# Scale and shift of a norm folded into the modulation behind it, and two moved steps in the MLP, in a two-layer transformer block kernel

## The reference

```python
y = concat(mixer) @ w_out
x = layer_norm(DEEPNORM_ALPHA * x + g_a * y, ln1_g, ln1_b)
h = x * (1 + sc_m) + sh_m
m = square(relu(h @ mlp_w1)) @ mlp_w2            # 1024 -> 4096 -> 1024
x = layer_norm(DEEPNORM_ALPHA * x + g_m * m, ln2_g, ln2_b)
```

## Time and profile before

| | us |
|---|---|
| runs, median (lowest to highest) | 3045.91 (3042.36 to 3052.49) |
| the profiled execution | 3046.93 |
| its span, first to last instruction | 3045.1 |
| PE busy | 2802.1 (92%) |
| DVE busy | 1397.4 (46%) |
| ACT busy | 878.6 (29%) |
| POOL busy | 559.6 (18%) |
| mean granted TensorE clock | 0.959 |

### The profile page before, as it was taken

The page is one execution under the profiler, slowest core; times in us unless marked ns, Lnnn a source line. Parts: engine busy times, 40 slices in busy tenths (PEclk is TensorE's granted clock), DMA queues, the critical chain, the costliest instruction groups (busy, mean ns, idle before and its releaser), DMA issues. The chain is left out here.

```text
span 3045.1 us, 40518 instructions
## 1 busy us (share of the span) xinstructions
PE 2802.1 (92%) x15572; PEld 2288.9 (75%) x15572; DVE 1397.4 (46%) x2153; ACT 878.6 (29%) x1684; POOL 559.6 (18%) x375
## 2 busy tenths in 40 slices
PE   5999993999999999999957999999698999999997
PEld 2666783778888888888845888888576888888886
DVE  3575435563333333333383555555555433333345
ACT  4243323342111121121224344343433211121222
POOL 0000002232112121121140000000033323233231
PEclk6999996999999999999977999999999999999999
DMA  6575214541101011010033111110356111111112
GB/s 219 195 301 166 73 52 158 165 132 49 35 28 55 28 41 41 28 55 28 30 122 96 42 36 49 36 36 8 105 131 173 48 46 44 55 41 41 55 41 56
DMA packets 192607, 238.90 MB, mean 78 GB/s; under 512 B 15960, under 2 KB 153776, under 8 KB 186352
## 3 DMA queue, kind: packets, MB, share of 16 engines
q1 hardware_dynamic: 192208, 237.29, 24.4%
q10 hardware_dynamic: 288, 0.10, 0.0%
HBM read 203.70 MB, written 37.88 MB: 79 GB/s over the span
## 5 line engine op out<-in xcount | busy, mean ns | idle before, releaser
L2054 DVE TENSOR_TENSOR y<-y,pair 128x1024 f32<-128x1024 f32 x280 | 340.1, 1219 | 314.1 <-PE pair L2161 314.1
L2159 PE MATMUL pair<-m_wbh,m_ath 128*128 128x512 f32 x1152 | 452.6, 393 | 15.0 <-DVE y L2054 8.4
L2161 PE MATMUL pair<-m_wbh,m_atl 128*128 128x512 f32 x1152 | 451.2, 392 | 0.0
L2160 PE MATMUL pair<-m_wbl,m_ath 128*128 128x512 f32 x1152 | 450.0, 391 | 0.0
L2103 DVE TENSOR_TENSOR m_atl<-m_sq,m_ath 128x512 fp32r<-128x512 f32 x160 | 138.4, 866 | 664.9 <-POOL m_sq L1972 664.0
L1932 ACT ACTIVATE m_rel<-pair 128x512 f32<-128x512 f32 x160 | 88.9, 556 | 996.7 <-PE pair L2183 986.3
L1972 POOL TENSOR_TENSOR m_sq<-m_rel 128x512 f32<-128x512 f32 x160 | 155.7, 973 | 1138.1 <-ACT m_rel L1932 1137.9
L2181 PE MATMUL pair<-hth,m0n_wah 128*128 128x512 f32 (+1 forms) x768 | 273.0, 355 | 2.8 <-ACT m_rel L1932 2.8
L2182 PE MATMUL pair<-htl,m0n_wah 128*128 128x512 f32 (+1 forms) x768 | 273.3, 356 | 0.0
L2183 PE MATMUL pair<-hth,m0n_wal 128*128 128x512 f32 (+1 forms) x768 | 273.2, 356 | 0.0
L2159 PEld LDWEIGHTS pair<-m_wbh,m_ath 128*128 128x128 f32 x1152 | 216.7, 188 | 70.1 <-DVE y L2054 16.8
(11 more groups left out here) (256 smaller groups left out, 5158.5 us busy)
## 6 DMA issues: line engine op xcount, KB each, us to landing
a_ring<-in_w_mod SPq DMA_DIRECT2D x40, 1024.0 KB, 9.1
m_rawb<-in_mlp_w SPq DMA_DIRECT2D x64, 512.0 KB, 4.2
m_rawa<-in_mlp_w SPq DMA_DIRECT2D x60, 512.0 KB, 4.2
x_rows<-r_res SPq DMA_DIRECT2D x28, 512.0 KB, 3.1
r_raw<-cat_cols SPq DMA_DIRECT2D x18, 512.0 KB, 6.0
mod_w<-in_w_mod SPq DMA_DIRECT2D x8, 1024.0 KB, 12.2
r_xin<-in_x SPq DMA_DIRECT2D x16, 512.0 KB, 3.6
gate_pre<-a0g_gout SPq DMA_DIRECT2D x20, 256.0 KB, 2.0
```

What stands on the lines that cost most here:

```text
L2054: dve.tensor_tensor(k.y[:, t, :], k.y[:, t, :], k.pair[t % 2][:, :], ALU.add).then_inc(s_y, 1)
L2159: pe.matmul(o, ath[:, m, ts], wbh[:, m, cols], start=m == 0, stop=False)
L2160: pe.matmul(o, ath[:, m, ts], wbl[:, m, cols], start=False, stop=False)
L2161: i = pe.matmul(o, atl[:, m, ts], wbh[:, m, cols], start=False, stop=m == M - 1)
```

## The change

The transposes no longer wait for POOL's two operations, but for the normed row alone, and the scale and shift of the norm are folded once per layer into the modulation's columns: scale' = (1 + sc) g, shift' = sh + (1 + sc) b. The two vectors are loaded as 16 rows, transposed by PE and applied by four small DVE operations. POOL still makes the row that is stored, but now in place only once the transposes have read it (a wait for `s_tr`). The last tile's transposes stand behind the first half of group 0 in `step(0)`. In layer 1 the first two `w2` pieces are loaded ahead of the rows of `y`, `begin_y` does two tiles ahead of the last `split_ht` instead of six, and POOL's gating stands ahead of all groups of a chunk. The last chunk of layer 1 leaves the loop: each group's `second(15, g)` follows its first product, with its `w2` parts in other buffers (`endh`, `endl`), and sums, squares and finishes are spread over both groups (four slots of `fmv` and `fstd` instead of two).

```diff
-        with eng.Fori(1, NCH) as c:
+        with eng.Fori(1, NCH - 1 if final else NCH) as c:
             body(c)
+        if final:
+            body(NCH - 1)
+
+    ends = lambda c: final and isinstance(c, int) and c == NCH - 1
+
+    def nth(c, t):
+
+        if not (final and isinstance(c, int) and c >= NCH - 2):
+            return tiles * c + t
+        g = [g for g in range(NG) if t in tiles_of(g)][0]
+        first, count = tiles_of(g)[0], len(tiles_of(g))
+        return tiles * (NCH - 2) + 2 * first + (c - (NCH - 2)) * count + t - first
...
+            for i, name in enumerate(("ln1_g", "ln1_b")):
+                sp.dma_start(lnr[i * KT:(i + 1) * KT, :], io[name][layer].rearrange("(k p) -> k p", p=P)).then_inc(s_lnr, 16)
...
+                    sp.wait_ge(s_dve, C * t + 2)
+                    for m in range(M):
+                        sp.dma_start(rawb[:, m, :], w2[m * P:(m + 1) * P, :]).then_inc(s_rawb[m], 16)
...
+                    if final and starts(c):
+                        continue
...
+                act.wait_ge(s_fold, 4)
...
+                if ends(c):
+                    act.wait_ge(s_alow, M * NCH)
+                    for m in range(M):
+                        act.wait_ge(s_bg, M * c + m + 1)
+                        act.activation(endh[:, m, :], rawb[:, m, :], ACT.Copy).then_inc(s_bhigh, 1)
...
-                    if g == NG - 1:
+                    if g == NG - 1 and not ends(c):
...
+                    if ends(c):
+                        act.wait_ge(s_sq, J * c + M * (g + 1))
+                        act.wait_ge(s_ath, J * c + M * (g + 1))
+                        for t in tiles_of(g):
+                            spread(t)
...
                 pool.wait_ge(s_dve, C * t + 6)
+                pool.wait_ge(s_tr, t + 1)
...
+                if final:
+                    for m in range(M):
+                        if starts(c):
+                            pool.wait_ge(s_grow, 16)
+                        wait(pool, s_rawb[m], 16 * (c + 1))
+                        pool.tensor_tensor(rawb[:, m, :], rawb[:, m, :], growt, ALU.mult).then_inc(s_bg, 1)
                 for g, (a, n) in enumerate(groups):
-                    if final and g == NG - 1:
-                        for m in range(M):
-                            if starts(c):
-                                pool.wait_ge(s_grow, 16)
-                            wait(pool, s_rawb[m], 16 * (c + 1))
-                            pool.tensor_tensor(rawb[:, m, :], rawb[:, m, :], growt, ALU.mult).then_inc(s_bg, 1)
...
+            scale, shift = [k.mod[:, layer, part * KT:(part + 1) * KT, :] for part in (SC_M, SH_M)]
+            column = lambda i: lnc[:, i, :].unsqueeze(2).broadcast_to([P, KT, 2])
+            dve.wait_ge(s_lnt, 1)
+            dve.tensor_copy(lnc[:, :, :].rearrange("p i j -> p (i j)"), k.bank[7][:, 0:2 * KT]).then_inc(s_fold, 1)
+            dve.wait_ge(s_fold, 1)
+            dve.tensor_tensor(lnt[:, :, :], scale, column(1), ALU.mult).then_inc(s_fold, 1)
+            dve.wait_ge(s_fold, 2)
+            dve.tensor_tensor(shift, shift, lnt[:, :, :], ALU.add).then_inc(s_fold, 1)
+            dve.tensor_tensor(scale, scale, column(0), ALU.mult).then_inc(s_fold, 1)
...
-            begin_y(0 if final else 2, XT - 2 if final else XT)
+            begin_y(0 if final else 2, 2 if final else XT)
             split_ht(tiles - 1)
-            begin_y(XT - 2 if final else XT, tiles)
+            begin_y(2 if final else XT, tiles)
...
+            def ending(c):
+                dve.wait_ge(s_lnrow, 32)
+                late = []
+                for g, (a, n) in enumerate(groups):
+                    for t in tiles_of(g):
+                        sum_tile(c - 1, t)
+                        if late and t > tiles_of(g)[0]:
+                            finish(late.pop(0))
+                    if g == 0:
+                        for m in range(M):
+                            dve.wait_ge(s_bhigh, M * c + m + 1)
+                            dve.tensor_tensor(endl[:, m, :], rawb[:, m, :], f32(endh[:, m, :]), ALU.subtract).then_inc(s_blow, 1)
+                    for m in range(M):
+                        j = J * c + g * M + m
+                        dve.wait_ge(s_sq, j + 1)
+                        dve.wait_ge(s_ath, j + 1)
+                        dve.tensor_tensor(atl[:, m, a:a + n], sq[:, m % 2, 0:n], f32(ath[:, m, a:a + n]), ALU.subtract).then_inc(s_atl, 1)
+                    for t in tiles_of(g):
+                        moments_sum(t)
+                        late.append(t)
+                        if len(late) > (2 if g < NG - 1 else 1):
+                            finish(late.pop(0))
+                for t in late:
+                    finish(t)
...
-                pe.wait_ge(s_b, t + 1)
+                pe.wait_ge(s_dve, C * t + 6)
...
+            pe.wait_ge(s_lnr, 32)
+            pe.transpose(k.bank[7][:, 0:2 * KT], lnr[:, :], k.ident[0:2 * KT, 0:2 * KT]).then_inc(s_lnt, 1)
...
-                        if g == 1:
-                            transposes(tiles - 1)
...
+                        if starts(c) and jj == 1:
+                            transposes(tiles - 1)
...
+                    if ends(c):
+                        second(c, g)
```

More of the change, by code:

```diff
@@ L1728, in stage_block @@
     s_dve, s_std, s_g, s_b, s_tr, s_mod, s_hh, s_hl, s_half = [rsem(x) for x in ("dve", "std", "g", "b", "tr", "mod", "hh", "hl", "half")]
+    s_lnr, s_lnt, s_fold = rsem("lnr"), rsem("lnt"), rsem("fold")
     s_store = [rsem(f"store{i}") for i in range(2)]
@@ L1934, in step, with spread @@
                         act.activation(ath[:, m, a:a + n], rel[:, m % 2, 0:n], ACT.Square).then_inc(s_ath, 1)
-            over_steps(act, step)
[L1936 to L1943, removed]
+                    if ends(c):
[3 more added lines that the diff above has]
+                            spread(t)
+            def spread(t):
+                act.wait_ge(s_mom, t + 1)
+                act.activation(rel[:, :, :].rearrange("p a b -> p (a b)"), k.y[:, t, :], ACT.Square, bias=fmv[:, t % 4, 0:1],
+                               accum_out=fmv[:, t % 4, 1:2]).then_inc(s_centre, 1)
+                act.wait_ge(s_centre, t + 1)
+                act.activation(fstd[:, t % 4, 0:1], fmv[:, t % 4, 1:2], ACT.Sqrt, bias=k.eps[:, 0:1], scale=1.0 / D).then_inc(s_fstd, 1)
+            over_steps(act, step)
         @block.gpsimd
@@ L2044, in _ @@
             split_ht(tiles - 2)
-            begin_y(0 if final else 2, XT - 2 if final else XT)
+            begin_y(0 if final else 2, 2 if final else XT)
             split_ht(tiles - 1)
-            begin_y(XT - 2 if final else XT, tiles)
+            begin_y(2 if final else XT, tiles)
             def sum_tile(c, t):
-                n = tiles * c + t
-                wait(dve, s_w2, n + 1)
-                wait(dve, s_y, n + 1)
+                wait(dve, s_w2, nth(c, t) + 1)
+                wait(dve, s_y, tiles * c + t + 1)
                 dve.tensor_tensor(k.y[:, t, :], k.y[:, t, :], k.pair[t % 2][:, :], ALU.add).then_inc(s_y, 1)
@@ L2069, in moments_sum @@
             def moments_sum(t):
-                n = tiles * (NCH - 1) + t
+                n = nth(NCH - 1, t)
                 dve.wait_ge(s_w2, n + 1)
-                dve.wait_ge(s_y, n + 1)
-                if t >= 2:
-                    dve.wait_ge(s_fstd, t - 1)
+                dve.wait_ge(s_y, tiles + nth(NCH - 2, t) + 1)
+                if t >= 4:
+                    dve.wait_ge(s_fstd, t - 3)
                 dve.tensor_tensor_reduce(k.y[:, t, :], k.y[:, t, :], k.pair[t % 2][:, :], 1.0, 0.0,
@@ L2077, in moments_sum @@
                 dve.wait_ge(s_y, tiles + n + 1)
[L2078 removed]
+                dve.tensor_scalar(fmv[:, t % 4, 0:1], stats[:, t % 2, 0, 0:1], -1.0 / D, None, ALU.mult).then_inc(s_mom, 1)
             def finish(t):
@@ L2082, in finish @@
                 dve.wait_ge(s_centre, t + 1)
-                dve.scalar_tensor_tensor(out=y, in0=y, scalar=fmv[:, t % 2, 0:1], in1=lng2, op0=ALU.add, op1=ALU.mult).then_inc(s_res, 1)
+                dve.scalar_tensor_tensor(out=y, in0=y, scalar=fmv[:, t % 4, 0:1], in1=lng2, op0=ALU.add, op1=ALU.mult).then_inc(s_res, 1)
                 dve.wait_ge(s_fstd, t + 1)
-                dve.reciprocal(fstd[:, t % 2, 1:2], fstd[:, t % 2, 0:1]).then_inc(s_frec, 1)
+                dve.reciprocal(fstd[:, t % 4, 1:2], fstd[:, t % 4, 0:1]).then_inc(s_frec, 1)
                 dve.wait_ge(s_frec, t + 1)
                 dve.wait_ge(s_res, t + 1)
-                dve.scalar_tensor_tensor(out=y, in0=y, scalar=fstd[:, t % 2, 1:2], in1=lnb2[:, :], op0=ALU.mult, op1=ALU.add).then_inc(s_fin, 1)
+                dve.scalar_tensor_tensor(out=y, in0=y, scalar=fstd[:, t % 4, 1:2], in1=lnb2[:, :], op0=ALU.mult, op1=ALU.add).then_inc(s_fin, 1)
             def step(c):
+                if ends(c):
+                    ending(c)
+                    return
                 for g, (a, n) in enumerate(groups):
@@ L2150, in second @@
```

(10 more changed lines are left out.)

12 lines of the change are left out of this document (5 added, 7 removed).

## The result

| | before | after |
|---|---|---|
| median of the runs, us | 3044.97 (3042.36 to 3052.49, 4 runs) | 3091.49 (3088.52 to 3093.74, 4 runs) |
| span of the profiled execution | 3045.1 | 3092.0 |
| mean granted clock | 0.959 | 0.951 |

A forecast was written before the change was run, and what follows sets the result against it. PE, busy 92% of the span, was taken as the bound. Terms 12.0 (layer 0) + 10.8 (layer 1) + 0.4 - 9.0 + 2.0 + 1.5 = +17.7 on 3046.9 gave 3064.6, stated as 3064 against the median; range 3035 to 3084.

The forecast's parts named there:

- the `w2` pieces: Layer 1, projection to MLP: two pieces loaded ahead of the rows of `y` bring the first second product earlier, -1.7 us.
- the held tiles: Projection: late low part held by POOL, tiles of 15.7 and 12.3 us, +1.9 a tile; 1.6 taken in layer 0.
- a rival of 20%: Projection: the held tiles lose the clock too, some 6 waits each with 2 us of slower matmuls, 3076 us; chance 20%.
- The wait behind the late load: Projection: input load issued 5.9 us behind the matmuls' start, landing 6.3 later in layer 1, 2.5 late; 1.0 in layer 0.
- One queue: Layer 1, projection's end: the rows of `y` are issued when DVE has taken the last product, moving with the projection.
- the `w1` pieces: First `w1` loads stand behind a store that waits for POOL and come late: +2 us in layer 0, +3 in layer 1.
- the hold: Projection: POOL's moved pair holds DVE's operations with two SBUF inputs, +1.3 us a tile.
- the gating: Chunks: gating as a chunk begins removes PE's waits of 0.6 us a chunk in 15 chunks, -9.0 us.
- the end: Last chunk: new order with two PE stalls of 2.8 us costs +2.0 us, plus 1.5 for the lower clock.
- the last transposes of layer 0: Layer 0, last tile: earlier transposes give back none to all of PE's 2.76 us wait; 1.2 taken.
- 3048: Rival "half of it": projection's hold shared out by slack, 0.7 us a tile, total 3048, no change; chance 12%.
- 3055: Rival "the hold alone": loads come in time, projection costs 12 x 1.3 = 15.6 us, total 3055; chance 15%.

The follow-up runs named there:

- experiment 3: The changed kernel with SP's store of a tile issued one step later, behind the next loads of input and residual: 3057.6 us, ratio 1.0043.
- experiments 8 to 11: Fold with POOL's own buffer: late `w2` 3041.2 us; late `w2`, old ending 3039.4; early `w2`, old ending 3034.9; late `w2`, old ending, chunk 0's old gating 3033.4.
- its twin: The changed kernel with POOL's result in its own buffer and the old order of the last chunk: 3034.9 us, ratio 0.9967.
- experiment 4: The changed kernel with POOL's result in a buffer of its own, not waiting for the transposes: 3035.2 us, ratio 0.9969; run again 3038.7, 0.9981.

## Why the prediction was wrong

The span grew by 46.9 where the sum had 17.7. The 29.2 between are, by the table and the parts below: 14.5 the clock, 9.6 the rest of the projection's tiles, 3.0 `growt`, 2.1 the `w2` pieces, 2.1 the stage starts, and -2.1 all the rest.

**The place named was right.** POOL's pair behind the transposes holds L2075 and makes the input's load late; the run without the fold shows no loss, the run with POOL elsewhere a gain. The Trainium skill ("SBUF — State Buffer", section "Who interferes with whom") has a DVE instruction with two inputs in SBUF and a GpSimd instruction that reads SBUF block each other, the later one in full. These rows agree: 3.04 on DVE, 3.25 on POOL.

**The step that failed is the clock behind the held tiles.** The forecast priced the tiles at 15.7 and 12.3 with every matmul at full rate, and put the lower clock into a rival of 20%, at 6 waits of 2 us. It happened in all seven tiles: 14.5 us by the matmuls, and by the run that fills the waits 13.5 of the projections' time and 10.6 of the whole in the medians. The prediction itself had said that 2.76 us of waiting cost the clock and that every other tile waits 3.6; the two together were the forecast, not a rival to it.

**The wait behind the late load was mis-sized in layer 1**, 7.9 of the 9.6. The load was given 6.3 us from issue to landing, from two landings; in layer 1's three late tiles 7.1 to 7.7 passed from issue to the copy (2256.39 to 2264.10, 2288.04 to 2295.36). It was also issued 6.8 behind the tile's first matmul, not 5.9 (2281.29 to 2288.04). Part of that is a misread row: before the change the load stood 0.6 us ahead of the matmuls (2248.70 against 2249.30), the 1.2 of the forecast is the store's time. So the low part came 3 us behind the start of POOL's pair and met its second operation, where the forecast had it meet the first: the waits of PE were 6.1, not 3.6. In layer 0 this part was right. The load took 4.9 to 5.4 us to the copy (4.8 given), the low part met the first operation, and PE waited 3.7. There the other 1.7 is the 1.6 a tile that was taken, where the 1.9 of the held tiles (7 x 1.9 = 13.3) gives about the 12.9 left without the clock.

**One queue was passed over.** The issue of `growt` and of the rows of `y` was said to move with the last product. It stands behind the store of tile 6, which waits for POOL. Layer 1 of the changed kernel:

```profile
2352.10 0.56 SPq L1848 DMA_DIRECT2D x_rows<-r_res  x1
2352.77 0.54 SPq L1836 DMA_DIRECT2D y<-gate_rows  x1
```

6.0 us behind where it stood, in place of the 3 put there for the `w1` pieces; with the store moved behind (experiment 3) it is back at 1.35.

**The `w2` pieces** gave +0.4, not -1.7. They were weighed against the kernel before alone; what they repay is the early gating of chunk 0 (4 us, experiments 8 to 11), which the forecast costed only for the later chunks. PE's wait there is now 8.54 for `wbl`, which POOL's squares hold to 4.04 for two.

**Right:** the hold (1.3 forecast, 0.9 measured alone), the gating (-9.0, measured -9.2), the end (+3.5, measured +3.0 here and 3.7 against its twin), with both stalls of PE near the size given (2.8 forecast):

```profile
3029.20 0.76 PE L2227 MATMUL pair<-m_endh,m_ath 128*128 128x512 f32 x1 [2.58 <-issue]
...
3067.60 0.47 PE L2227 MATMUL pair<-m_endh,m_ath 128*128 128x512 f32 x1 [2.58 <-issue]
```

The first stall lost the clock (its first matmul takes 0.76, and the 7 us behind it read 0.76 granted), the second did not (0.47, and 1.00).

**Better than forecast:** the last transposes of layer 0. They were to give back 1.2 and the late `w1` pieces to take 2; the stretch fell by 1.3 in all, and by 2.9 in experiment 4, where nothing is late.

**A slip in the rivals:** the forecast goes by the median before (3045.9), but 3048 and 3055 add their sums to the profiled execution (3046.9). By the median they are 3047 and 3054. It decides nothing here.

Open: why the stage starts cost 2.5 us for two small loads. Over the kernels with the fold, first load to first matmul in layer 1 ranged from 8.1 to 9.8 against 8.0, and no run separated it. Open too is why the same load takes longer in layer 1 (7.1 to 7.7) than in layer 0 (4.9 to 5.4).

## What to carry to other kernels

A step taken off a chain has to be put somewhere: list what its engine meets there, and every issue that a queue holds behind it, before counting the gain. A buffer of its own for the moved result gave the gain that the new order alone turned into a loss. Where a forecast adds a wait on PE of a size that the trace already shows losing the clock, the slower matmuls belong in the sum, not beside it.

## What the runs showed that was not expected

Useless matmuls paid: 128 of them in one execution (56 in layer 0, 72 in layer 1) took 10.6 us off; behind two of the waits of 6.1 us the next 7 us had stood at a granted clock of 0.60 and 0.75. A stall of 2.58 us lost the clock once and kept it once in the same execution.

DVE's products, with one input in PSUM, were not held: in experiment 3 two of them took 1.28 us inside a POOL operation (2273.63 to 2276.59), where the residual right behind, with both inputs in SBUF, took 2.11 for 1.23. That POOL operation took 2.96 for its usual 2.40, but not for the products: it began 0.71 us before the end of the low part L2030 (2273.11 to 2274.34), which has both inputs in SBUF.
